# All 16384 experts' scores on TensorE, value rows alone gathered, both blocks in pairs of tiles

## The reference

```
s1 = einsum('thd,kd->thk', q[..., :half], keys_1)       # 128 keys per half and head
s2 = einsum('thd,kd->thk', q[..., half:], keys_2)
v1, i1 = top_k(s1, 16);  v2, i2 = top_k(s2, 16)
cand = v1[..., :, None] + v2[..., None, :]              # 256 candidates per head
sc, ci = top_k(cand, 16)
eidx = i1[ci // 16] * 128 + i2[ci % 16]                 # 128 experts per token
gates = softmax(sc)
act = gelu(einsum('td,tkd->tk', x, peer_u[eidx]))       # 128 dots of length 1024 per token
y   = einsum('tk,tkd->td', gates * act, peer_v[eidx])   # weighted sum of 128 rows
```

## Time and profile before

| | |
|---|---|
| median of 3 runs | 3166.22 us (3160.13 to 3168.16) |
| profiled execution | 3159.39 us, span 3158.1 us |
| busy: PE / DVE / ACT / POOL | 2272.4 / 1802.2 / 426.0 / 1432.2 us |
| granted clock of TensorE, mean | 0.81 |
| moved by DMA | 829.57 MB, mean 263 GB/s |
| by the gathers' queue / SyncE's queue | 539.99 MB / 283.19 MB |

### The profile page before, as it was taken

How to read it: one execution, slowest core, us unless ns; L and a number is a source line. 1 busy time by engine, 2 the same in 40 slices (tenths; PEclk the granted TensorE clock), 3 DMA queues, 4 the chain that set the end, 5 groups by cost and what they waited for, 6 DMA issues and landing times. The chain is left out here.

```text
span 3158.1 us, 24727 instructions
## 1 busy us (share of the span) xinstructions
PE 2272.4 (72%) x8222; PEld 1376.0 (44%) x8222; DVE 1802.2 (57%) x3876; ACT 426.0 (13%) x1209; POOL 1432.2 (45%) x1137
## 2 busy tenths in 40 slices
PE   5997980056673784767674478979957687969989
PEld 3535850023432662322344235758425443437544
DVE  1512119978779677566477897674666854224300
ACT  1212000011200100000000232012000321013310
POOL 0000002377667787778767764676655433100000
PEclk9796995577695796999885557989977688987999
DMA  3310522599889999978889877999998779942376
GB/s 129 121 67 27 173 96 101 157 350 370 282 337 329 333 401 352 321 237 266 293 306 398 288 249 230 394 386 393 363 360 330 259 246 379 340 153 83 126 259 220
DMA packets 291759, 829.57 MB, mean 263 GB/s; under 512 B 23568, under 2 KB 30016, under 8 KB 290864
## 3 DMA queue, kind: packets, MB, share of 16 engines
q0 software_dynamic: 148464, 539.99, 47.7%
q1 hardware_dynamic: 139872, 283.19, 24.7%
q10 hardware_dynamic: 3296, 4.80, 0.4%
HBM read 825.81 MB, written 2.10 MB: 262 GB/s over the span
## 5 line engine op out<-in xcount | busy, mean ns | idle before, releaser
L315 POOL DMA_INDIRECT picks_rows<-peer_u_dram,expert x512 | 723.5, 1413 | 830.2 <-DVE expert L1465 516.2
L315 POOL DMA_INDIRECT picks_rows<-peer_v_dram,expert x512 | 618.1, 1207 | 477.4 <-DVE h L380 354.6
L374 DVE CUSTOM_DVE_ANT_0 picks_rows<-picks_rows,xn 128x1024 f32<-128x1024 f32 x512 | 613.7, 1223 | 169.0 <-DMA picks_rows<-peer_u_dram,expert 144.4
L380 DVE SCALAR_TENSOR_TENSOR h<-picks_rows,picks_weight,h 128x1024 f32<-128x1024 f32 x416 | 535.0, 1286 | 189.4 <-DMA picks_rows<-peer_v_dram,expert 116.3
L465 PE MATMUL psum<-weight_ring,hnT 128*128 128x512 f32 (+4 forms) x576 | 236.9, 573 | 23.0 <-DMA weight_ring<-w_in_dram 10.9
L403 PE MATMUL psum<-picks_rows,picks_diag 128*128 128x512 f32 x384 | 187.3, 625 | 59.9 <-POOL picks_diag L333 59.5
L1753 PE MATMUL psum<-weight_ring,aT 128*128 128x512 f32 x512 | 220.8, 593 | 3.1 <-ACT aT L2060 1.4
L465 PEld LDWEIGHTS psum<-weight_ring,hnT 128*128 128x128 f32 (+1 forms) x576 | 106.2, 187 | 152.4 <-issue 137.5
L874 PE MATMUL psum<-identity_sb,na_probs 128*128 128x128 f32 (+2 forms) x384 | 93.7, 359 | 100.9 <-DVE na_probs L958 79.4
L656 PE MATMUL psum<-identity_sb,n_scaled 128*128 128x128 f32 (+1 forms) x104 | 24.1, 412 | 181.9 <-DVE n_scaled L640 181.9
L1753 PEld LDWEIGHTS psum<-weight_ring,aT 128*128 128x128 f32 x512 | 96.9, 190 | 125.3 <-issue 120.5
(11 more groups left out here) (353 smaller groups left out, 3170.8 us busy)
## 6 DMA issues: line engine op xcount, KB each, us to landing
weight_ring<-w_ff_dram SPq DMA_DIRECT2D x48, 2048.0 KB, 11.0
weight_ring<-w_in_dram SPq DMA_DIRECT2D x44, 2048.0 KB, 13.6
weight_ring<-w_proj_nsa_dram SPq DMA_DIRECT2D x6, 2048.0 KB, 8.1
weight_ring<-w_out_dram SPq DMA_DIRECT2D x6, 2048.0 KB, 14.8
weight_ring<-w_ret_out_dram SPq DMA_DIRECT2D x4, 2048.0 KB, 8.0
weight_ring<-w_mix_out_dram SPq DMA_DIRECT2D x4, 2048.0 KB, 18.9
weight_ring<-w_peer_q_dram SPq DMA_DIRECT2D x4, 2048.0 KB, 13.4
picks_rows<-peer_u_dram,expert POOLq DMA_INDIRECT x512, 7.8
```

The lines of the kernel that those rows point to most:

```text
L315: pool.indirect_dma_start(out=self.rows[:, n % GATHERS, :], out_offset=None, in_=table, in_offset=bass.IndirectOffsetOnAxis(ap=self.expert ...
L374: ins = nc.vector.tensor_tensor_reduce(out=row, in0=row, in1=self.x[t], scale=1.0, scalar=0.0, op0=ALU.mult, op1=ALU.add, accum_out=self.d ...
L380: ins = nc.vector.scalar_tensor_tensor(out=h, in0=row, scalar=self.weight[:, t % 2, k:k + 1], in1=h, op0=ALU.mult, op1=ALU.add)
```

## The change

Instead of gathering `peer_u` rows, TensorE computes the score of every expert for every token. `peer_u` is stored in HBM as 32 slabs of 512 experts (`SLABS`). A new `experts_stage` stands at the end of each first wave, in place of the two `sel` stages. In it TensorE does 8 matmuls of 512 columns for each slab and tile; ScalarE copies the 128 x 512 scores to one of four staging buffers and issues a DMA that stores them to an HBM tensor (128 x 16384 floats for a tile); VectorE does the selection of both tiles beside that. The key products of the second tile stand behind slab 7, its exponentials behind the last store.

GpSimd then waits for all stores of the stage and gathers, per pick, one 4-byte score per token (L302 of the new kernel) straight into `dots`, and 4 KB value rows as before (L312). The scores of a pair's first tile all stand ahead of its first value row; those of its second tile alternate with the first tile's value rows. The dots on VectorE, the diagonals on GpSimd and the sum on TensorE are gone: VectorE adds all 512 value rows, so there are 512 steps, with a new `SHARES` table. Steps begin in `ma3_1` (the attention for tile 3 in the second first-block wave). PSUM banks for products are 8 instead of 6.

The second block runs in two waves of two tiles (`SECOND = ((0, 2), (2, 4))`), so its weights are loaded twice instead of three times. The last wave has no steps beside it.

```diff
-SECOND = ((0, 2), (2, 3), (3, 4))
+SECOND = ((0, 2), (2, 4))
-BANKS = 6
-V_BANKS = (6, 7)
+BANKS = 8
 SHARES = {
+    "ma3_1": 10, "rp_1": 22, "tr_1": 3, "re_1": 17, "rn_1": 4, "m1_1": 41, "mix_1": 12, "np_1": 5, "pq_1": 12, "ex_1": 130,
+    "na2_0": 41, "m2_0": 41, "out2_0": 12, "n32_0": 5, "ff12_0": 54, "ff22_0": 96, "nf2_0": 7}
...
+        one += [(("pu", c), a["peer_u"][c], n) for c in range(SLABS)]
...
+    def issue(self, pool, tiles, stored):
+        for signal in stored:
+            pool.wait_ge(*signal)
+        self.gather_scores(pool, tiles[0], range(PICKS))
+        for t in tiles:
+            for k in range(PICKS):
+                self.gather_values(pool, t, k)
+                if t + 1 in tiles:
+                    self.gather_scores(pool, t + 1, range(k, k + 1))
+    def gather_scores(self, pool, t, picks):
+        for k in picks:
+            if k == 0:
+                pool.wait_ge(self.expert_ready, t + 1)
             pool.indirect_dma_start(
+                out=self.dots[:, t, k:k + 1], out_offset=None, in_=self.scores[t],
+                in_offset=bass.IndirectOffsetOnAxis(ap=self.place[:, t, k:k + 1], axis=0),
+            ).then_inc(self.dots_landed[t], 16)
+    def gather_values(self, pool, t, k):
+        n = PICKS * t + k
+        if n >= GATHERS:
+            pool.wait_ge(self.taken, n - GATHERS + 1)
...
     def activate(self, act, turn=None):
         limit = self.last if turn is None else self.after(turn)
+        while self.activated < NT and self.activated * PICKS < limit:
+            t = self.activated
+            act.wait_ge(self.dots_landed[t], 16 * PICKS)
...
+        def tensor(pe):
+            g.begin(pe)
+            for c, name in enumerate(names):
+                if c == 0:
+                    keys(pe, 0)
+                if c == next_keys and n > 1:
+                    keys(pe, 1)
+                w = g.w.view(name)
+                g.w.arrived(pe, name)
+                for j in range(n):
+                    i = n * c + j
+                    if i >= 4:
+                        pe.wait_ge(*s_copied.after(i - 3))
+                    for k in range(KT):
+                        mm = nc.tensor.matmul(bank(i), xnT[:, k, P * j:P * j + P], w[:, k, :], start=(k == 0), stop=(k == KT - 1))
+                    mm.then_inc(g.w.products_done, 1)
...
+                    act.wait_ge(g.w.products_done, g.w.product(name, j))
+                    if i >= STAGES:
+                        act.wait_ge(*s_stored[i % STAGES].after(16 * (i // STAGES)))
+                    nc.scalar.copy(staged[:, i % STAGES, :], bank(i)).then_inc(s_copied.sem, 1)
+                    act.wait_ge(*s_copied.after(i + 1))
+                    rows = g.picks.scores[t].rearrange("(p e) o -> p (e o)", p=P)
+                    act.dma_start(rows[:, 512 * c:512 * c + 512], staged[:, i % STAGES, :]).then_inc(s_stored[i % STAGES].sem, 16)
```

More of the change, by code:

```diff
@@ L267, with __init__ @@
 class Picks:
-    def __init__(self, g, ctx, peer_u, peer_v, expert, gates):
+    def __init__(self, g, ctx, peer_v, scores, expert, place, gates):
         nc, self.g = g.nc, g
@@ L359, in use_to @@
     def use_to(self, dve, end):
-        nc = self.g.nc
         while self.used < end:
             n = self.used
-            t, table, k = self.steps[n]
-            if table is not self.peer_u and self.weights == t:
-                if t:
-                    self.fold(dve, t - 1)
+            t, k = n // PICKS, n % PICKS
+            if self.weights == t:
                 self.make_weights(dve, t)
             self.used += 1
-            if self.owner[n] == "pe":
-                continue
-            row = self.rows[:, n % GATHERS, :]
@@ L382, in use_to @@
-            ins.then_inc(self.taken["dve"], 1)
-    def add(self, pe, turn=None):
-        self.add_to(pe, self.last if turn is None else self.after(turn - 1))
-    def add_to(self, pe, end):
-        nc = self.g.nc
-        while self.added < end:
-            n = self.added
-            self.added += 1
-            if self.owner[n] != "pe":
-                continue
-            t, _, k = self.steps[n]
-            at = self.number[n] - 1
-            mine = [m for m in range(PICKS) if on_pe(t, m)]
-            if k == mine[0] and self.sums[t]:
-                pe.wait_ge(self.sum_added, self.sums[t])
-            pe.wait_ge(self.landed[n % GATHERS], 16 * (n // GATHERS + 1))
-            pe.wait_ge(self.diag_ready, at + 1)
-            for c, bank in enumerate(V_BANKS):
-                mm = nc.tensor.matmul(self.g.psum[:, bank, :], self.diag[:, at % DIAGS, :],
-                                      self.rows[:, n % GATHERS, 512 * c:512 * c + 512], start=(k == mine[0]), stop=(k == mine[-1]))
-            mm.then_inc(self.taken["pe"], 1)
@@ L1132, in tensor @@
             mm.then_inc(s_turned.sem, 1)
-        g.picks.add(pe)
     def scalar(act):
@@ L1410, in tensor, with sync @@
                     rows = slice(64 * half, 64 * half + 64)
-                    mm = nc.tensor.matmul(scores(2 * h + half), pqT[rows, h, columns], keysT[rows, :],
-                                          start=True, stop=True)
+                    mm = nc.tensor.matmul(key_scores(2 * h + half), pqT[rows, h, P * j:P * j + P], keysT[rows, :], start=True, stop=True)
             mm.then_inc(s_scores.sem, 1)
-            g.picks.add(pe)
+        def sync(sp):
+            g.w.load_through(sp, names[-1])
```

298 lines of the change are left out of this document (121 added, 177 removed), and 6 rows, old and new, of the table SHARES.

## The result

The kernel after took 3369.55 us (median of 4 runs, 3362.74 to 3375.93), the kernel before 3163.18 beside it; the ratio is 1.066, 95% interval 1.062 to 1.071. The profiled execution's span was 3371.4 us. The stages of the new trace, cut at the bounds that the prediction names; the columns are those of the earlier trace rows.

The account below looks back on a forecast made before the run. No engine bounds the kernel throughout; the question was whether TensorE's new work fits its 886 idle us. Serial stages sum 470 + 447 + 13 + 523 + 450 + 25 + 736 + 25 + 661 = 3350 us, range 3190 to 3460.

Parts of the forecast that it names:

- 1 first wave to `pq_0`: From the start to the end of `pq_0`: nothing changes, 470 us.
- 9 last pair: Second block's last two tiles together, without steps beside them: 661 us.
- Items 2, 3, 5, 6: Two experts stages, 447 and 450 us, and the hand-overs behind them, 13 and 25 us.
- Item 4: Second first-block wave, 523 us: 448 without steps, plus 40 for steps, 20 waiting for first dots, 15 for pairs.
- Items 7 and 8: Second block's first pair, 736 us, with 285 for its MLP by bytes; then final and next norm, 25 us.
- Rival A: Steps hide nearly whole and TensorE paces the first pair's MLP: about 3230 us; chance 0.17.
- Rival B: GpSimd's gather pace binds both waves; at 1.55 us each, 63 us more, twice: 3475 us; chance 0.10.
- the other rule cited: DMA transfers under 512 bytes are read, modified and written; 512 score gathers could take zero to 664 us, near zero taken.
- Rival C: TensorE's idle time goes almost entirely: 3145 us with no step exposed, 3100 with a higher clock; chance 0.10.
- Rival D: TensorE waits in the experts stages for slabs or ScalarE's stores; both 10% slower cost 90 us, 3440; chance 0.05.
- in short: Two experts stages bring 897 us, of which 144 + 270 replace other time; waves get back 141 + 60 + 175, under 483.
- its signs: Expected in the new profile: hand-over idle under 15 us, dots wait 10 to 30, gathers 1.3 to 1.5, MLP idle some 60.

Follow-up runs that it names:

- e1: The kernel after with all gathers and all steps on the residual left out, experts stages and stores kept: 3073.4 us, ratio 0.973 to the kernel before.
- e2: The kernel after without the 512 score gathers, gelu reading other data: 3239.9 us, ratio 1.026 to the kernel before.
- e3: The kernel after with value rows of 2 KB instead of 4 KB, each used in two adds of 512: 3325.1 us, ratio 1.053 to the kernel before.
- e9: The kernel after without score gathers and with value rows of 2 KB, both together: 3224.3 us, ratio 1.020 to the kernel before.
- e10: The kernel after with experts' products in bfloat16 and 36 steps moved from the second first-block wave into the second experts stage: ratio 1.069 to the kernel before.

## Why the prediction was right, step by step

The forecast was 3350 us in a range of 3190 to 3460, and the direction slower; measured were 3369.6. Its nine items against the trace:

| item | forecast | measured |
|---|---|---|
| 1 first wave to `pq_0` | 470 | 468.3 |
| 2 first experts stage | 447 | 443.9 |
| 3 hand-over | 13 | 12.3 |
| 4 second first-block wave | 523 | 533.4 |
| 5 second experts stage | 450 | 443.9 |
| 6 hand-over | 25 | 22.5 |
| 7 and 8 first pair of the second block, hand-over | 761 | 795.1 |
| 9 last pair | 661 | 652 |

**Items 2, 3, 5, 6.** The price of a matmul from a stretch of pure products, times the count, gave both experts stages within 6 us. The wait for the last store was 5.1 us where 4 was taken.

**Item 4** is right in sum and wrong in its parts. The base was 31 us too high: without a step the wave takes 417 us (`e1`), not 448. The steps cost 34 (`e2` against `e1`, 451 less 417), 40 forecast. The score gathers cost 82 (`e2` against the kernel after), where the wait and the pairs had 20 and 15. The wait alone was 52.6: the scores of tile 0 took GpSimd 165 us (918.4 to 1083.6; 170 forecast), but ScalarE came to the gelu 122 us after the last store, not 150. The errors cancelled, and that the item comes within 10 us is luck.

**Items 7 and 8.** To the end of the attention 292 us were measured, 299 forecast, with a wait of 12.9 us for tile 2's dots where 12 was taken. Merge, output and norm took 176 in place of 152, and the MLP with the hand-over 327 in place of 310. The 285 us for the MLP rested on bytes alone, and the prediction's own sign of some 60 us of idle TensorE behind it came out at 103. GpSimd had been late since the experts stage: between 1909 and 2527 its score gathers and pairs follow one another almost without a wait. In the second half of the MLP the rows then landed 13.8 us (median) after their issue, with DMA at 401 GB/s, and 6.8 us behind the last weight. GpSimd's timeline with free DMA engines, twice in that half, and behind the last weight; then one of VectorE's steps there:

```profile
1083.56 0.94 POOL L312 DMA_INDIRECT picks_rows<-peer_v_dram,expert  x1 [0.30 <-issue]
...
2563.27 0.94 POOL L312 DMA_INDIRECT picks_rows<-peer_v_dram,expert  x1 [1.11 <-DVE h L354]
2565.32 0.93 POOL L312 DMA_INDIRECT picks_rows<-peer_v_dram,expert  x1 [1.12 <-DVE h L354]
...
2606.69 1.74 POOL L312 DMA_INDIRECT picks_rows<-peer_v_dram,expert  x1 [0.30 <-issue]
2608.74 1.74 POOL L312 DMA_INDIRECT picks_rows<-peer_v_dram,expert  x1 [0.31 <-issue]
...
2654.14 1.08 POOL L312 DMA_INDIRECT picks_rows<-peer_v_dram,expert  x1 [0.30 <-issue]
```

```profile
2608.38 1.28 DVE L354 SCALAR_TENSOR_TENSOR h<-picks_rows,picks_weight,h 128x1024 f32<-128x1024 f32 x1 [0.76 <-DMA picks_rows<-peer_v_dram,expert]
```

The gathers start 2.04 to 2.05 us apart in both pairs of rows, whether they take 0.94 or 1.74 us. At 2563 GpSimd has all eight buffers out and waits 1.1 us until a step gives one back, and the step waits for its row. So the rows' landing sets the pace there, and not GpSimd's issue. With 58 gathers in the 113 us from 2504 to 2617, at a DMA share of 1.04, the 96 steps of the table could not be taken there; `e3` and `e9` show the rest of the tail to be VectorE's own steps.

**Rival A** (steps hide nearly whole, 3230) is excluded: 294 us of delay are left. **Rival B** had its mechanism in part: from 1909 on GpSimd issues 512 gathers in about 790 us, 1.54 each, which is the pace at which B decides, but most of that time has cover, and the wave and the pair end 10 and 34 us over the forecast, not 63 each. The prediction weighed the Trainium skill's "GPSIMD Engine Reference", section "Specifications", on the SBUF interfaces shared with VectorE. The trace agrees: in the kernel after, 441 gathers that no value step overlapped took 0.96 us on the mean and 583 that one overlapped 1.25, and of the 197 among these over 1.3 us, 195 ended 0.79 to 0.84 us after the end of a step. The rows above show it: the step from 2608.38 ends at 2609.66, the gather from 2608.74 at 2610.48. In the kernel before 388 of 398 long ones do the same. It goes with VectorE's instruction and not with the load of the DMA engines: the gathers of 0.94 us at 2563 stand at a DMA share of 1.03, and with the half-length adds of `e3` no score gather took over 1.50. Beside steps the means of 16 were 1.0 to 1.4 us before the MLP, so the slow price of the earlier trace rows was not the mean. What this contention costs the kernel in time no run shows; without it GpSimd would be busy some 170 us less of 1150, by estimate from the 0.96. On 4-byte packets the other rule cited did not decide anything: by the 0.024 us a gather under `e2`, the 512 score gathers kept the 16 engines busy for about 12 us, near the lower end of the 0 to 664 that the prediction gave. **Rival C** put the floor at 3145 or 3100; it is 3073 (`e1`). Its attentions were too dear: without steps they take 55 and 103 us, the second even at clock 0.57. It still loses, since the steps are not hidden; no table tried here hides them all. **Rival D** is excluded by the trace: TensorE was busy 443.7 and 443.8 of 444 us, so no experts stage waited for slabs or stores.

The sum of the whole is thus: floor + 578, made of two stages of 456 and 466 us for selections of 118 and 126, less 101 in the second block; delay - 370; together + 208, against 206 measured. The mechanism of the forecast, two stages of products that replace less than they cost, is shown. Its closeness is partly luck: the prediction's own floor (rival C) was 3145 and its delays 205, measured were 3073 and 296, so the one was 72 too high and the other 91 too low. Its sentence "in short" doesn't add up either: what the first pair gets back by its own items is 38 us (774 less 736) and not 60, and the three hand-overs of items 3, 6 and 8, 63 us, are left out there. The sum of the nine items is right.

Of its signs, the records and the clock of the experts stages, the first hand-over, GpSimd's cadence, the DMA share in the MLP and the last pair came out. The second hand-over (22.5 for under 15), the wait for dots in `ma3_1` (44.4 for 10 to 30) and the idle time behind the MLP did not.

## What to carry to other kernels

When work moves to an engine that looks idle, price it with a floor of each kernel (all side work left out): here the idle 886 us were waits in places that the new work could not fill, and 578 us of floor bought 370 of delay. A gather costs its queue nearly as much for 4 bytes a row as for 4 KB (1.04 and 1.21 us), so trading the `peer_u` rows for scores left 530 of their 724 us of GpSimd standing. Before a stage is filled with side work, look for slack at its end (52 us of idle VectorE here), and expect the slack to be gone once the stage itself is made shorter. When a run leaves out one thing, check that it leaves the other engines' work alone: half rows made each of VectorE's steps 0.2 us longer, and the tail that was left was theirs.

## What the runs showed of the hardware

- A gather of 128 x 4 bytes occupied GpSimd for 1.04 us on the mean, one of 128 x 4 KB for 1.21; with no value step beside it either took 0.94 to 0.96. Where the queue did not wait, 0.30 us lay between two.
- A gather that runs into a VectorE step with two SBUF inputs ends just after it: 195 of 197 long ones (over 1.3 us) ended 0.79 to 0.84 us after a step's end. Beside single steps of 1.28 us in the MLP a gather took 1.74. At a DMA share of 1.03 gathers clear of the steps still took 0.94.
- With 8 buffers and DMA at 401 GB/s, rows of 128 x 4 KB landed 13.8 us (median) after issue and 2.04 us apart; with the weights loaded 6.8 us.
- 4-byte gathers hardly loaded the DMA engines: 109 of them kept GpSimd's queue busy 1.9% of the 16 engines' time over 138 us.
- Two adds of 128 x 512 took VectorE 1.49 us where one of 128 x 1024 took 1.28 (in a row 1.51 and 1.37).
- TensorE kept clock 1.00 over 444 us of float32 products, beside DMA at 408 GB/s.
- Where they were full (share 1.0 and over) the core's DMA engines moved 394 to 421 GB/s, in the mixtures of slabs, stores and rows seen here.
- ScalarE's cast of 128 x 4096 floats to bfloat16, in place, took 3.60 us; with bfloat16 matmuls of 512 columns in place of float32 ones the first experts stage took 211 us in place of 444, at a DMA share of 0.95.
- In one kernel's executions on one chip (`e10`) all engines but GpSimd nearly stood during both bursts of 128 score gathers, and its four runs took 3364 to 3418 us where the same kernel took 3076 to 3090 on another; not explained.
